# Gates through DRAM, attention A between the gate products, attention B with transposed scores

## The chip, the cores and the metric

One Trainium2 chip, one core. The metric is the device time of one execution in microseconds; the kernel before is given by the median of three runs.

## What is computed

One residual block, 1024 positions of 1024 numbers, float32. Cut to what matters here:

```python
h = rms_norm(x, g_mix[l])
z = h @ w_in[l]
qa, ka, va, cq, ckv, krope, gates = jnp.split(z, COL_SPLITS, axis=-1)
y_a = swa_sink_attention(...)     # 8 heads of 64, 2 kv heads, window of 2 chunks of 64, sinks
y_b = mla_attention(...)          # 8 heads, q and k of 96, v of 64, chunk-causal softmax over all keys
gt = jax.nn.sigmoid(gates + b_gate[l])                       # two gates of 1024 columns
merged = gt[:, :, 0] * (y_a @ w_branch_a[l]) + gt[:, :, 1] * (y_b @ w_branch_b[l])
x = x + merged @ w_out[l]
x = x + jnp.square(jax.nn.relu(rms_norm(x, g_mlp[l]) @ w_ff1[l])) @ w_ff2[l]
```

## The kernel before

Every engine has a program written out by hand, and semaphores join them. The large products are split: each float32 operand is a high and a low part in fp32r, and `split_products` (L1001) makes three products of them. GpSimd splits the weights (`split`, L583 and L585), ScalarE and VectorE the activations.

The stages follow one another on TensorE. (1) x is normalised and transposed, and z is made in four column chunks. (2) 16 gate tiles of 128 columns, 48 products of 128x512 each, in two pairs of PSUM banks; ScalarE's sigmoid (L831, L842) writes all of them to `gate`, 64 KB per partition of SBUF, and between the first eight it squares z for the norms. (3) 18 groups of four transposes (L1008) make `qaT`, `kaT`, `cqT`, `ckvT`. (4) Attention A: 16 units, one per query tile and kv head: scores (L1138), `maxima` on VectorE (L1513 to L1521), exps on ScalarE (L902), normalisation on GpSimd (L693), transposes of P (L1163), values (L1190). Unit k's scores stand beside unit k-1's transposes and unit k-2's values. (5) Attention B: 64 units, one per head and query tile n: scores of n+1 key tiles in plain f32 (L1148), row maximum (L1529), exp (L908), n+1 transposes of P (L1167, L1174), n+1 products with V (L1194), the division by the row sum (L1560). The heads go in groups of two; `group_step` (L1110, L1112, L1008) projects and transposes q and k of a group, one step in each unit, one group ahead, with GpSimd scaling and rotating (L592, L660 to L685). (6) yB is transposed, and `branches` (L1001) makes 8 pairs of branch tiles of 24 products; VectorE's `merge` multiplies by the gates. (7) Output projection, second norm, feed-forward in 8 groups.

Orders are fixed by the loops over k in each engine's program. The softmax of B subtracts an exact row maximum, per query row on a partition.

## Time and profile before

| | us |
|---|---|
| median of 3 runs (lowest, highest) | 1498.99 (1498.45, 1500.33) |
| profiled execution | 1497.08 |
| its span | 1495.1 |
| TensorE busy | 1439.5 |
| VectorE, ScalarE, GpSimd busy | 533.4, 361.3, 502.3 |
| first branch product starts at | 608.1 |

The span runs from the first to the last instruction of the profiled execution, and the execution's own time is 2.0 us more. A busy TensorE can be one whose products follow each other at less than their best pace, so starts are read beside durations. The granted clock of the span is 0.992 of 2.4 GHz.

### The profile page before, as it was taken

The page shows a single profiled execution, that of the slowest core. Times are in us where ns is not written, and L with a number is a line of the kernel's source. Part 1 is how long each engine was busy: PE and PEld are TensorE (multiplying, and loading weights), DVE is VectorE, ACT ScalarE, POOL GpSimd, SP SyncE. Part 2 cuts the span into 40 slices and gives each one's busy share as a digit, 9 for nine tenths or more (in the row PEclk, how much of TensorE's full clock was granted, in tenths as well). Part 3 has the DMA queues.
Part 4 walks back from the last instruction along what each step waited for, and adds up shares of the span by engine and source line. Part 5 has one row for each costly group of instructions (what it writes and reads, how often), then busy time and mean ns, then how long its engine had stood idle before and what let it go on. Part 6 is the DMA issues. An engine that isn't in the chain of part 4 may idle for free.

```text
span 1495.1 us, 18639 instructions
## 1 busy us (share of the span) xinstructions
PE 1439.5 (96%) x7304; PEld 1202.3 (80%) x7304; DVE 533.4 (36%) x980; ACT 361.3 (24%) x781; POOL 502.3 (34%) x357
## 2 busy tenths in 40 slices
PE   7999999977699999899999999999999999999998
PEld 6998888865488877788888888888888888888887
DVE  5300115068666665555253222122222222222212
ACT  5112211065455554210032102020110202011020
POOL 2330654117243241125407133150513415051320
PEclk9999999998999999999999999999999999999999
DMA  7120121000010000015202112030211203021112
GB/s 228 31 57 14 43 56 42 14 23 1 18 38 2 1 1 29 16 55 181 87 1 81 47 43 71 4 95 14 70 42 39 73 0 98 14 70 42 30 40 98
DMA packets 78390, 71.43 MB, mean 48 GB/s; under 512 B 6784, under 2 KB 69760, under 8 KB 78336
## 3 DMA queue, kind: packets, MB, share of 16 engines
q1 hardware_dynamic: 78192, 70.19, 15.7%
q8 instruction: 34, 0.56, 0.1%
q10 hardware_dynamic: 144, 0.52, 0.1%
q14 instruction: 20, 0.16, 0.0%
HBM read 66.51 MB, written 4.19 MB: 47 GB/s over the span
## 4 chain that ended last, share of the span: by engine, by line
PE 89%; DVE 3%; ACT 2%; issue 2%; POOL 2%; DMA 1%; ACTq 0%; SPq 0%; DVEq 0%; POOLq 0%
PE PS L1001 75%; PE PS L1194 4%; PE PS L1148 4%; PE PS L1008 2%; PE PS L1167 2%; PE PS L1110 1%; ACT scA L902 1%; POOL scA L693 1%; DVE uT_lo L1658 1%; PE PS L1112 1%; PE PS L1174 1%; DMA z_raw<-in_w_in 0%; PE PS L1163 0%; DVE yT_lo L1586 0%; ACT uT_hi L989 0%
## 5 line engine op out<-in xcount | busy, mean ns | idle before, releaser
L583 POOL TENSOR_SCALAR w_hi<-raw 128x1024 fp32r<-128x1024 f32 x64 | 74.5, 1164 | 407.5 <-PE PS L1001 406.1
L1658 DVE TENSOR_TENSOR uT_lo<-relu_sq,uT_hi 128x512 fp32r<-128x512 f32 x64 | 92.4, 1479 | 278.6 <-ACT uT_hi L989 278.6
L975 ACT ACTIVATE relu_t<-PS 128x512 f32<-128x512 f32 x64 | 34.8, 595 | 553.3 <-PE PS L1001 553.3
L1664 DVE TENSOR_TENSOR xr<-PS,xr 128x1024 f32<-128x1024 f32 x64 | 78.4, 1225 | 245.6 <-PE PS L1001 245.6
L585 POOL TENSOR_TENSOR w_lo<-raw,w_hi 128x1024 fp32r<-128x1024 f32 x64 | 159.7, 2496 | 5.3
L1001 PE MATMUL PS<-mT_hi,w_hi 128*128 128x512 f32 x512 | 160.3, 389 | 0.7 <-POOL w_lo L585 0.7
L1001 PE MATMUL PS<-mT_lo,w_hi 128*128 128x512 f32 x512 | 160.3, 389 | 0.0
L1001 PE MATMUL PS<-mT_hi,w_lo 128*128 128x512 f32 x512 | 160.2, 389 | 0.0
L1001 PE MATMUL PS<-w_hi,uT_hi 128*128 128x512 f32 x512 | 158.4, 391 | 1.7 <-DVE uT_lo L1658 1.7
L1001 PE MATMUL PS<-w_lo,uT_hi 128*128 128x512 f32 x512 | 157.8, 389 | 0.0
L1001 PE MATMUL PS<-w_hi,uT_lo 128*128 128x512 f32 x512 | 157.6, 389 | 0.0
L1001 PEld LDWEIGHTS PS<-w_hi,uT_hi 128*128 128x128 f32 x512 | 95.6, 188 | 24.0 <-DVE uT_lo L1658 3.9
L1001 PEld LDWEIGHTS PS<-mT_hi,w_hi 128*128 128x128 f32 x512 | 96.1, 188 | 20.7 <-issue 0.9
L1001 PEld LDWEIGHTS PS<-w_lo,uT_hi 128*128 128x128 f32 x512 | 96.1, 188 | 20.1
L1001 PEld LDWEIGHTS PS<-w_hi,uT_lo 128*128 128x128 f32 x512 | 96.1, 188 | 20.0
L1001 PEld LDWEIGHTS PS<-mT_hi,w_lo 128*128 128x128 f32 x512 | 96.1, 188 | 20.0
L1001 PEld LDWEIGHTS PS<-mT_lo,w_hi 128*128 128x128 f32 x512 | 96.1, 188 | 19.9
L1001 PE MATMUL PS<-hT_hi,gw_hi 128*128 128x512 f32 x256 | 79.0, 389 | 0.5 <-ACT Zr L797 0.5
L1194 PEld LDWEIGHTS PS<-vB,ptB 128*128 128x128 f32 x576 | 71.3, 191 | 9.7 <-ACT ptB L921 6.4
L1001 PE MATMUL PS<-hT_lo,gw_hi 128*128 128x512 f32 x256 | 78.8, 389 | 0.0
L1001 PE MATMUL PS<-hT_hi,gw_lo 128*128 128x512 f32 x256 | 78.8, 389 | 0.0
L1001 PE MATMUL PS<-zw_hi,hT_hi 128*128 128x320 f32 (+1 forms) x256 | 77.9, 304 | 0.0
(194 smaller groups left out, 2384.8 us busy)
## 6 DMA issues: line engine op xcount, KB each, us to landing
raw<-in_w_ff SPq DMA_DIRECT2D x64, 512.0 KB, 3.8
g_raw<-in_w_in SPq DMA_DIRECT2D x16, 512.0 KB, 3.8
x_in<-in_x SPq DMA_DIRECT2D x8, 512.0 KB, 10.7
raw<-in_w_out SPq DMA_DIRECT2D x8, 512.0 KB, 3.5
xr<-in_x SPq DMA_DIRECT2D x8, 512.0 KB, 7.6
out<-xr SPq DMA_DIRECT2D x8, 512.0 KB, 2.6
z_raw<-in_w_in SPq DMA_DIRECT2D x4, 640.0 KB, 8.1
z_raw<-in_w_in SPq DMA_DIRECT2D x4, 544.0 KB, 3.8
```

The costliest lines, as they stand in the source:

```text
L583: pool.tensor_scalar(hi_ap, raw_ap, 1.0, 1.0, ALU.mult, ALU.mult).then_inc(hi_done, 1)
L585: pool.tensor_tensor(lo_ap, raw_ap, hi_ap, ALU.subtract).then_inc(ready, 1)
L693: pool.tensor_tensor(p, p, bcast(r, [P, A_GROUP, WIN]), ALU.mult).then_inc(p_normed, 1)
L902: ins = act.activation(scA[:, s, g, 0:WIN + 1], scA[:, s, g, 0:WIN + 1], ACT.Exp, bias=a_nmax[:, s, g:g + 1], accum_out=a_sum[:, ss, g:g + 1])
L975: act.activation(relu_t[:, cols], PS[:, 2 * (j % 2) + h, :], ACT.Relu).then_inc(relu_ready, 1)
L1001: ins = pe.matmul(o, st, cut(mv), start=first and n == 0, stop=last and n == 2)
L1008: ins = pe.transpose(PS[0:rows, bank, i * P:(i + 1) * P], ap, ident[:, :])
L1148: ins = pe.matmul(pair(2 * s)[:, c:c + w], qbT[gs][0:QK, h, n * P:(n + 1) * P], kbT[gs][0:QK, h, c:c + w], start=True, stop=True)
L1167: ins = pe.transpose(PS[:, 4, c * P:(c + 1) * P], prB[s][:, c * P:(c + 1) * P], ident[:, :])
L1194: ins = pe.matmul(PS[:, 6, 0:V_DIM], ptB[s][:, c, :], vB[(m // B_GROUP) % 3][:, c, m % B_GROUP, :], start=c == 0, stop=c == n)
L1658: dve.tensor_tensor(uT_lo[:, j, cols], relu_sq[:, cols], uT_hi[:, j, cols], ALU.subtract).then_inc(uT_ready, 1)
L1664: dve.tensor_tensor(xr[:, t, :], pair(4 + 2 * (t % 2)), xr[:, t, :], ALU.add).then_inc(x3_added, 1)
```

## The change

Two stages are woven and one is turned.

- **Gates through DRAM.** `gate` is two buffers of 4 KB per partition; SP stores each tile to `gate_store` in DRAM and fetches it back for the branches. From the fifth gate tile on all use one pair of PSUM banks (`gate_pair`), so the others are free for what is woven in.
- **Attention A and the first head group lie between the gate products.** The 16 gate tiles are cut into 64 points of 12 products. After a point come two small transposes (points 18 to 26), a step of A (28 to 46), a step of the first group (47 to 59) or three approximate scores of head 0 (60 to 63).
- **Attention B in slots.** A head has 12 slots: query half 0 with key tiles 0 to 3, half 1 with key tiles 0 to 7. `scores_t` makes scores with keys on partitions and up to 512 queries along the row, as three fp32r products of split q and k; a 97th row (ones in k, the negative row maximum in q) subtracts the maximum. Exp writes P in the layout that `values_t` takes, so nothing is transposed: V (with a column of ones, which gives the row sums) is the weights, P is moved. The maxima come a head ahead from `approx`, a single fp32r product in the natural layout, through `row_max` and four DMAs that lay a column of 128 numbers into a row. Per half the row sums go by DMA to a column, VectorE takes reciprocals, and two DMAs spread them through DRAM to 64 rows.
- **Branches.** The 16 tiles go in the order `ORDER`, with four of A first, one tile of 24 products each. yB needs no transposes.

The core of the diff:

```diff
--- before.py
+++ after.py
...
-N_B = B_HEADS * T
-N_UNITS = N_A + N_B
-BG_UNITS = B_GROUP * T
+Q_BLOCK = 4
+BLOCKS = B_HEADS * T // Q_BLOCK
+HEAD_SLOTS = Q_BLOCK + T
+N_SLOTS = B_HEADS * HEAD_SLOTS
+P_RING = 3
+S_RING = 2
+KQ_RING = 4
+SC_RING = 3
+BW_RING = 4
+POINTS = 4
+SMALL_AT = 18
+A_AT = 28
+PROJ_AT = 47
+TURN_AT = 56
+SHIFT_AT = 60
...
+        def gate_pair(u):
+
+            return 0 if u in (1, 3) else 5
+
...
+        def a_step(p):
+
+            return p - A_AT if 0 <= p - A_AT < N_A + 3 else None
+
+        def first_group(p):
+
+            if 0 <= p - PROJ_AT < T:
+                return [p - PROJ_AT]
+            if 0 <= p - TURN_AT < T // 2:
+                return [T + 2 * (p - TURN_AT), T + 2 * (p - TURN_AT) + 1]
+            return []
+
+        def first_chunks(p):
+
+            q = p - SHIFT_AT
+            return [3 * q, 3 * q + 1, 3 * q + 2] if 0 <= q < N_CHUNKS // 3 else []
+
...
+        def preparations(t):
+
+            h, r = t // HEAD_SLOTS, t % HEAD_SLOTS
...
+            def nmax_move(u):
+
+                h, half = u // 2, u % 2
+                with nc.allow_non_contiguous_dma(reason="128 numbers from a column to a row"):
+                    for i in range(Q_BLOCK):
+                        n = Q_BLOCK * half + i
+                        if half == 0:
+                            sp.wait_ge(approx_read, N_CHUNKS * h + i + 1)
+                        else:
+                            sp.wait_ge(nmax_ready, Q_BLOCK * h + i + 1)
+                        sp.dma_start(qT_hi[h % KQ_RING][QK:QK + 1, n * P:(n + 1) * P].bitcast(F32), b_nmax[:, u % 2, i:i + 1]
+                                     ).then_inc(nmax_landed[u % 2], 16)
...
+            def sum_move(u):
+                sp.wait_ge(y_raw_ready, u + 1)
+                sp.dma_start(b_sum[:, u % 2, :], sum_row(u).rearrange("o (p t) -> o p t", t=Q_BLOCK)
+                             ).then_inc(sum_landed[u % 2], 16)
+
+            def reciprocal_spread(u):
+                s, r = u % 2, V_DIM * ((u // 2) % 2)
+                sp.wait_ge(rsum_b_ready, u + 1)
+                sp.dma_start(r_d[s], b_rsum[:, s, :]).then_inc(r_stored, 16)
+                sp.wait_ge(r_stored, 16 * (u + 1))
+                sp.dma_start(r_row[s][r:r + V_DIM, :],
+                             r_d[s].rearrange("p t -> (p t)").rearrange("(o q) -> o q", o=1).partition_broadcast(V_DIM)
+                             ).then_inc(r_landed[s], 16)
...
+            def exp_b(t):
+                h, half, kt, c0 = slot(t)
+                act.wait_ge(st_done, t + 1)
+                before = p_tile_before(t)
+                if before >= 0:
+                    act.wait_ge(slot_done, before + 1)
+                p, sc = p_tile(t), PS[:, 2 + t % S_RING, :]
+                if diagonal(t):
+                    act.activation(p[0:CHUNK, c0:c0 + CHUNK], sc[0:CHUNK, c0:c0 + CHUNK], ACT.Exp)
+                    act.activation(p[:, c0 + CHUNK:HALF], sc[:, c0 + CHUNK:HALF], ACT.Exp).then_inc(p_ready, 1)
                 else:
...
+            def y_out(u):
+
+                odd = (u // 2) % 2
+                act.wait_ge(slot_done, block_end(u))
+                if u >= 2:
+                    act.wait_ge(yB_ready, u - 1)
+                dst, src = y_raw[u % 2], PS[:, 5 + u % 2, :]
+                if odd:
+                    act.activation(dst[0:1, :], src[V_DIM:V_DIM + 1, :], ACT.Copy)
+                    act.activation(dst[V_DIM:P, :], src[0:V_DIM, :], ACT.Copy).then_inc(y_raw_ready, 1)
+                else:
...
+            def y_high(u):
+
+                h, half = u // 2, u % 2
+                rows, cols = slice(V_DIM * (h % 2), V_DIM * (h % 2) + V_DIM), slice(half * HALF, (half + 1) * HALF)
+                act.wait_ge(y_normed, u + 1)
+                act.activation(yT_hi[4 + h // 2][rows, cols], y_raw[u % 2][rows, :], ACT.Copy).then_inc(yB_hi_done, 1)
...
+            def approx(a):
+
+                h, n, c, w = chunk(a)
+                q, k = qT_hi[h % KQ_RING], kT_hi[h % KQ_RING]
+                if n == 0 and h % B_GROUP == 0:
+                    pe.wait_ge(qk_ready, T * (h // B_GROUP + 1))
+                if a == 0:
+                    pe.wait_ge(max_ready, N_A)
+                if a >= 2:
+                    pe.wait_ge(approx_read, a - 1)
+                pe.matmul(PS[:, a % 2, 0:w], q[0:QK, n * P:(n + 1) * P], k[0:QK, c:c + w], start=True, stop=True
+                          ).then_inc(approx_done, 1)
+
+            def scores_t(t):
+
+                h, half, kt, c0 = slot(t)
+                s = h % KQ_RING
+                keys, cols = slice(kt * P, (kt + 1) * P), slice(half * HALF + c0, (half + 1) * HALF)
+                if t == 0:
+                    pe.wait_ge(k_one_ready, KQ_RING)
+                if kt == 0:
+                    u = 2 * h + half
+                    pe.wait_ge(nmax_landed[u % 2], 16 * Q_BLOCK * (u // 2 + 1))
+                if t >= S_RING:
+                    pe.wait_ge(p_ready, t - S_RING + 1)
+                out = PS[:, 2 + t % S_RING, c0:HALF]
+                pe.matmul(out, kT_hi[s][0:QK + 1, keys], qT_hi[s][0:QK + 1, cols], start=True, stop=False)
+                pe.matmul(out, kT_hi[s][0:QK, keys], qT_lo[s][0:QK, cols], start=False, stop=False)
+                pe.matmul(out, kT_lo[s][0:QK, keys], qT_hi[s][0:QK, cols], start=False, stop=True
+                          ).then_inc(st_done, 1)
+
+            def values_t(t):
+
+                h, half, kt, c0 = slot(t)
+                u, g = 2 * h + half, h // B_GROUP
+                last = t + 1 == block_end(u)
+                pe.wait_ge(p_ready, t + 1)
+                if kt == 0 and u >= 2:
+                    pe.wait_ge(y_raw_ready, u - 1)
+                if t % (2 * HEAD_SLOTS) == 0 and g < 3:
...
+                    pe.wait_ge(p_zero_ready, Q_BLOCK)
+                ins = pe.matmul(out[:, c0:HALF], vB[g % 3][:, kt, h % B_GROUP, :], p_tile(t)[:, c0:HALF],
+                                start=kt == 0, stop=last)
+                ins.then_inc(slot_done, 1)
+
+            def gate_chunks(u, q):
+                b = gate_pair(u)
+                if q == 0:
+                    pe.wait_ge(gw_ready, u + 1)
+                    before = [v for v in range(u) if gate_pair(v) == b]
+                    if before:
+                        pe.wait_ge(gate_ready, before[-1] + 1)
+                for k in range(2 * q, 2 * q + 2):
+                    ins = split_products(gw_hi[u % 2][:, k, :], gw_lo[u % 2][:, k, :], hT_hi[:, k, :], hT_lo[:, k, :],
+                                         [(PS[:, b + h, :], halves[h]) for h in range(2)], k, k == 0, k == KD - 1)
+                if q == POINTS - 1:
+                    ins.then_inc(gate_done, 1)
+
+            for p in range(2 * KD * POINTS):
+                gate_chunks(p // POINTS, p % POINTS)
+                for n in small_at(p):
+                    small_transpose(n)
+                k = a_step(p)
+                if k is not None:
+                    if 2 <= k < N_A + 2:
+                        p_transposes(k - 2, 0)
+                    if k < N_A:
+                        scores(k)
+                    if k >= 3:
+                        values(k - 3)
+                    if 2 <= k < N_A + 2:
+                        p_transposes(k - 2, 1)
+                for q in first_group(p):
+                    group_step(0, q)
+                for a in first_chunks(p):
...
+            for t in range(N_SLOTS):
+                scores_t(t)
+                if t >= 2:
+                    values_t(t - 2)
+                a = chunk_at(t)
+                if a is not None:
+                    approx(a)
+                for g, p in preparations(t):
+                    group_step(g, p)
+            values_t(N_SLOTS - 2)
+            values_t(N_SLOTS - 1)
...
+            def row_max(a):
+
+                h, n, c, w = chunk(a)
+                u, i = 2 * h + n // Q_BLOCK, n % Q_BLOCK
+                dve.wait_ge(approx_done, a + 1)
+                if u >= 2 and i == 0 and c == 0:
+                    dve.wait_ge(nmax_landed[u % 2], 16 * Q_BLOCK * (u // 2))
+                sc = PS[:, a % 2, 0:w]
+                if c + w == (n + 1) * P:
+                    link(dve, dve.memset(sc[0:CHUNK, w - CHUNK:w], -MASKED))
+                out = b_nmax[:, u % 2, i:i + 1]
...
+            def y_norm(u):
+                rows, _ = block_rows(u)
+                dve.wait_ge(r_landed[u % 2], 16 * (u // 2 + 1))
+                dve.tensor_tensor(y_raw[u % 2][rows, :], y_raw[u % 2][rows, :], r_row[u % 2][rows, :], ALU.mult
+                                  ).then_inc(y_normed, 1)
+
+            def y_low(u):
+                rows, cols = block_rows(u)
+                j = 4 + u // 4
+                dve.wait_ge(yB_hi_done, u + 1)
+                dve.tensor_tensor(yT_lo[j][rows, cols], y_raw[u % 2][rows, :], yT_hi[j][rows, cols], ALU.subtract
+                                  ).then_inc(yB_ready, 1)
...
```

Where the instructions move, at three places.

TensorE in attention A: a unit before (transposes of P from `scA`, scores from `qaT` and `kaT`, a projection of the first group, values from `ptA`).

```order
L1190 MATMUL PS<-ptA,v_even 128x256 [waits y_ready,pt0_ready]
L1190 MATMUL PS<-ptA,Zr 128x256
L1163 MATMUL PS<-ident,scA 128x64 [waits p_normed,pt0_ready,exp_done]
L1163 MATMUL PS<-ident,scA 128x64 x7
L1138 MATMUL PS<-kaT,qaT 128x192 [waits max_ready]
L1138 MATMUL PS<-kaT,qaT 128x192 x3
L1110 MATMUL PS<-wuq,cqT 128x192 [waits proj_dve_read,proj_act_read]
L1110 MATMUL PS<-wuq,cqT 128x192
```

Now, the same unit, with a point of gate products (`gw` times `hT`) behind it.

```order
L1375 MATMUL PS<-ident,scA 128x64 [waits p_normed,pt0_ready,exp_done]
L1375 MATMUL PS<-ident,scA 128x64 x3
L1360 MATMUL PS<-kaT,qaT 128x192 [waits max_ready]
L1360 MATMUL PS<-kaT,qaT 128x192 x3
L1389 MATMUL PS<-ptA,v_even 128x256 [waits y_ready,pt0_ready]
L1389 MATMUL PS<-ptA,Zv 128x256
L1375 MATMUL PS<-ident,scA 128x64 [waits pt_half]
L1375 MATMUL PS<-ident,scA 128x64 x3
L1245 MATMUL PS<-hT_hi,gw_hi 128x512 x2
L1245 MATMUL PS<-hT_lo,gw_hi 128x512 x2
L1245 MATMUL PS<-hT_hi,gw_lo 128x512 x2
```

The projections have left the unit, the transposes are two halves around scores and values, and gate products stand before the next.

ScalarE in attention A before: projections' reads, `ptA`, exps.

```order
L902 ACTIVATE scA,a_sum<-scA,a_nmax 128x193 [waits max_ready]
L902 ACTIVATE scA,a_sum<-scA,a_nmax 128x193 x3
L879 ACTIVATE q_nat<-PS 128x192 [waits proj_done]
L882 ACTIVATE sqB<-PS 128x448 [waits b_summed]
L917 ACTIVATE ptA<-PS 128x512 [waits pt0_done]
L902 ACTIVATE scA,a_sum<-scA,a_nmax 128x193 [waits max_ready]
```

Now, around the end of a gate tile.

```order
L1118 ACTIVATE scA,a_sum<-scA,a_nmax 128x193 [waits max_ready]
L1118 ACTIVATE scA,a_sum<-scA,a_nmax 128x193 x3
L1048 ACT_TABLE_LOAD [waits gate_stored1]
L1048 ACTIVATE gate<-PS,b_gate_c 128x1024 [waits gate_done]
L1126 ACTIVATE ptA<-PS 128x512 [waits pt0_done]
L1118 ACT_TABLE_LOAD
L1118 ACTIVATE scA,a_sum<-scA,a_nmax 128x193 [waits max_ready]
L1118 ACTIVATE scA,a_sum<-scA,a_nmax 128x193 x3
L1126 ACTIVATE ptA<-PS 128x512 [waits pv_done,pt0_done]
```

A sigmoid stands between the exps of two units, with a table load ahead of it and one behind.

SP's queue in attention B, of a head (before, it held nothing there but the loads of two weights a group).

```order
L649 DMA b_sum<-y_raw 128x1x4 [waits y_raw_ready]
L639 DMA qT_hi<-b_nmax 1x128x1 [waits approx_read] x4
L655 DMA r_store<-b_rsum 128x4 [waits rsum_b_ready]
L657 DMA r_row<-r_store 64x512 [waits r_stored]
L639 DMA qT_hi<-b_nmax 1x128x1 [waits nmax_ready] x4
L649 DMA b_sum<-y_raw 128x1x4 [waits y_raw_ready]
L655 DMA r_store<-b_rsum 128x4 [waits rsum_b_ready]
L657 DMA r_row<-r_store 64x512 [waits r_stored]
L649 DMA b_sum<-y_raw 128x1x4 [waits y_raw_ready]
```

VectorE at the same time, one half block.

```order
L1823 TENSOR_REDUCE b_part<-PS 128x1 [waits nmax_landed1,approx_done]
L1832 RECIPROCAL b_rsum<-b_sum 128x4 [waits r_stored,sum_landed1]
L1817 MEMSET PS 64x64 [waits approx_done]
L1823 TENSOR_REDUCE b_part<-PS 128x1 [waits dve_step]
L1826 TENSOR_TENSOR b_nmax<-b_part 128x1 [waits approx_read]
L1823 TENSOR_REDUCE b_part<-PS 128x1 [waits approx_done]
L1842 TENSOR_TENSOR y_raw<-y_raw,r_row 64x512 [waits r_landed1]
L1817 MEMSET PS 64x64 [waits approx_done]
L1823 TENSOR_REDUCE b_part<-PS 128x1 [waits dve_step]
```

The maxima, the sums and the reciprocals of a head all go through SP in this order, and VectorE's multiply by `r_row` stands in its queue ahead of later row maxima.

## Rows read from the trace of the kernel before

**Rows 1.** The page: busy time, and the chain that ended last by engine.
```profile
PE 1439.5 (96%) x7304; PEld 1202.3 (80%) x7304; DVE 533.4 (36%) x980; ACT 361.3 (24%) x781; POOL 502.3 (34%) x357
...
PE 89%; DVE 3%; ACT 2%; issue 2%; POOL 2%; DMA 1%; ACTq 0%; SPq 0%; DVEq 0%; POOLq 0%
```

**Rows 2.** Windows, four stages; columns: width, then busy us (instructions) per engine, clock, DMA.
```profile
127.00:301.40 174.40, 174.25 (x769) 144.23 (x770) 33.93 (x95) 29.32 (x36) 69.97 (x32) 1.00 0.14 36
301.40:401.20 99.80, 69.72 (x478) 51.37 (x476) 74.21 (x199) 58.03 (x183) 43.36 (x44) 0.90 0.05 13
401.20:601.50 200.30, 196.17 (x1293) 161.39 (x1293) 121.53 (x406) 105.48 (x253) 62.20 (x70) 0.99 0.05 15
...
608.10:1495.10 887.00, 880.17 (x3904) 726.98 (x3904) 262.18 (x214) 127.54 (x234) 289.52 (x164) 1.00 0.18 55
```

**Rows 3.** Timeline, TensorE, attention A; columns: start us, us, line, operation, idle before.
```profile
312.85 1.65 PE L1138 MATMUL PS<-kaT,qaT 64*128 64x192 f32 x8 [2.02 <-DVE ckvT L1439]
...
341.85 0.47 PE L1163 MATMUL PS<-ident,scA 64*128 64x64 f32 x8 [1.03 <-POOL scA L693]
...
343.26 0.89 PE L1110 MATMUL PS<-wuq,cqT 128*128 128x192 f32 x4 [0.23 <-DVE vB L1476]
...
346.61 0.47 PE L1163 MATMUL PS<-ident,scA 64*128 64x64 f32 x8 [0.90 <-POOL scA L693]
```

**Rows 4.** Timeline, TensorE: z stage, small transposes, attention B, output products.
```profile
119.86 0.29 PE L1001 MATMUL PS<-zw_lo,hT_hi 128*128 128x272 f32 x1
119.99 0.28 PE L1001 MATMUL PS<-zw_hi,hT_lo 128*128 128x272 f32 x1
...
301.38 1.91 PE L1008 MATMUL PS<-ident,Zq 128*128 128x128 f32 x16
303.12 1.04 PE L1008 MATMUL PS<-ident,k_dup 128*128 128x128 f32 x8
...
560.40 0.66 PE L1167 MATMUL PS<-ident,prB 128*128 128x128 f32 x4 [0.55 <-ACT prB L908]
...
577.25 1.88 PE L1148 MATMUL PS<-kbT,qbT 96*128 96x512 f32 x4
578.97 0.56 PE L1194 MATMUL PS<-vB,ptB 128*128 128x64 f32 x4
...
581.95 0.66 PE L1167 MATMUL PS<-ident,prB 128*128 128x128 f32 x4 [0.55 <-ACT prB L908]
...
775.00 0.71 PE L1001 MATMUL PS<-ow_hi,mT_hi 128*128 128x512 f32 x2
```

**Rows 5.** Groups by line and shape, 110 to 610 us; busy us, mean ns of one.
```profile
L585 POOL TENSOR_TENSOR gw_lo<-g_raw,gw_hi 128x1024 fp32r<-128x1024 f32 x14 | 33.9, 2424 | 1.2
...
L902 ACT ACTIVATE scA<-scA,a_nmax 128x193 f32<-128x193 f32 x64 | 28.2, 444 | 0.0
...
L592 POOL TENSOR_TENSOR b_rstd<-b_ms,minus_half 128x16 f32<-128x16 f32 x8 | 23.3, 2913 | 90.9 <-DVE b_ms L1500 90.9
...
L1529 DVE TENSOR_REDUCE b_nmax<-PS 128x1 f32<-128x512 f32 x8 | 5.5, 691 | 0.3
```

**Rows 6.** Timeline, ScalarE, around the first gate tile.
```profile
138.44 1.28 ACT L831 ACT_TABLE_LOAD   x1 [9.51 <-PE PS L1001]
139.73 1.12 ACT L831 ACTIVATE gate<-PS,b_gate_c 128x1024 f32<-128x1024 f32 x1
```

**Rows 7.** DMA issues (KB, us to landing), then SP's queue (start, us of issue).
```profile
raw<-in_w_ff SPq DMA_DIRECT2D x64, 512.0 KB, 3.8
...
pos_i<-in_positions SPq DMA_DIRECT2D x1, 4.0 KB, 14.2
...
g_ckv_c<-in_g_ckv SPq DMA_DIRECT2D x1, 0.5 KB, 2.2
...
7.60 3.21 SPq L463 DMA_DIRECT2D pos_i<-in_positions  x1
...
20.92 0.47 SPq L463 DMA_DIRECT2D g_ckv_c<-in_g_ckv  x1
```

More of the change, by code:

```diff
@@ L302, in build @@
         g_mlp_in = sem("g_mlp_in")
-        xr_landed = [sem(f"xr_landed{t}") for t in range(T)]
         o_done = sem("o_done")
@@ L397, in kind @@
         def kind(k):
[L399 to L415 removed]
+            return k // 2, k % 2
         def yT_cols(k, odd):
[L419 removed]
+            m, n = kind(k)
             rows = slice(CHUNK * odd, CHUNK * odd + CHUNK)
@@ new lines, in scores @@
+                    pe.wait_ge(max_ready, k - 1)
+                for g in range(A_GROUP):
+                    head = A_GROUP * n + g
+                    r = A_DIM * (head % 2)
+                    ins = pe.matmul(PS[:, 2 * s + g % 2, 256 * (g // 2):256 * (g // 2) + WIN],
+                                    qaT[r:r + A_DIM, head // 2, m * P:(m + 1) * P],
+                                    kaT[r:r + A_DIM, n, m * P:m * P + WIN], start=True, stop=True)
+                ins.then_inc(qk_done, 1)
@@ new lines, in scores_t @@
+            def scores_t(t):
+                h, half, kt, c0 = slot(t)
+                s = h % KQ_RING
[12 more added lines that the diff above has]
+                          ).then_inc(st_done, 1)
@@ L1241, in out_tile @@
+            for e in range(2 * KD):
+                branch(e)
             def out_tile(n):
@@ L1417, in _ @@
             dve.wait_ge(rope_ready, 2)
-            with dve.Fori(0, T // 2) as i:
+            for i in range(T // 2):
                 z_norms(i, False)
@@ new lines, in maxima @@
+                if k == 0:
+                    dve.wait_ge(dist_ready, 3)
+                if k >= SC_RING:
+                    dve.wait_ge(pt0_done, k - SC_RING + 1)
+                for g in range(A_GROUP):
+                    dve.scalar_tensor_tensor(out=sc[:, g, 0:WIN], in0=dist[:, m, :],
+                                             scalar=-SLOPES[A_GROUP * n + g],
+                                             in1=PS[:, 2 * s + g % 2, 256 * (g // 2):256 * (g // 2) + WIN],
+                                             op0=ALU.mult, op1=ALU.add)
@@ new lines, in _ @@
+            dve.wait_ge(gate_done, 2 * KD)
+            for i in range(2, KQ_RING):
+                dve.memset(kT_hi[i][QK:QK + 1, :].bitcast(F32), 1.0).then_inc(k_one_ready, 1)
+            for i in range(Q_BLOCK):
+                dve.memset(p_diag[i][CHUNK:P, i * P:i * P + CHUNK], 0.0).then_inc(p_zero_ready, 1)
+            for t in range(N_SLOTS):
+                a = chunk_at(t)
+                if a is not None:
+                    row_max(a)
+                for g, p in preparations(t):
+                    group_vec(g, p)
+                for u in range(BLOCKS):
+                    if t == block_end(u) + 4:
+                        sum_reciprocal(u)
+                    if t == block_end(u) + 6:
+                        y_norm(u)
+                    if t == block_end(u) + 8:
+                        y_low(u)
@@ L1611, in x2_norm, with merged_low @@
+            def merged_low(d):
+                dve.wait_ge(mT_hi_done, d + 1)
+                dve.tensor_tensor(mT_lo[:, d, :], gate_b[:, d, :], mT_hi[:, d, :], ALU.subtract).then_inc(mT_ready, 1)
+            for e in range(2 * KD):
+                gate_multiply(e)
+                if ORDER[e][0] and ORDER[e][1]:
+                    merged_low(ORDER[e][1] - 1)
+            merged_low(KD - 1)
             def x2_norm(t):
```

1074 lines of the change are left out of this document (555 added, 519 removed).

## The prediction, made before the change was run

> **What bounds the kernel now.** I read the page first: TensorE is busy 96% of the span, and the chain that ended last lies on it for 89% [rows 1]. So the time changes only by work taken off TensorE or by gaps on it. The stages say where gaps are [rows 2]: the gate products (127 to 301 us) and all from the branch products to the end (608.1 to 1495.1 us) are full, while attention A fills 69.7 of 99.8 us at a mean granted clock of 0.90, and attention B fills 196.2 of 200.3 us. The timeline of A shows the gap [rows 3]: transposes of one unit start at 341.85 and of the next at 346.61, so a unit takes 4.76 us, with about 1 us of it idle until GpSimd's normalisation (L693) is done. After a wait of 2.02 us the scores take 1.65 us, where transposes and scores together otherwise take 1.4 (341.85 to 343.26): that is the lower of the two clocks, 1.2 GHz.
>
> From the end of the z stage to the first branch product before is 608.1 - 127.0 = 481.1 us [rows 2]. All of the change falls there. From 608.1 on, the same number of products at the same shapes is left (887 us), and I cost that at nothing: gates come back from DRAM as 16 loads of 512 KB under 87 us of products; such a load lands in 3.8 us [rows 7].
>
> **Prices of TensorE's work.** Split products (fp32r) of 512 columns: 174.4 us hold 769, so 0.2267 us each [rows 2]. Of 272 columns: 0.125 us from start to start [rows 4]. Both are N/2.4 ns and 12 ns more, so I take 0.173 for 384 and 0.120 for 256. For 128 there is no row; between 0.066 (this formula) and 0.11 (a full-rate transpose: 16 in 1.74 us [rows 4]) I take 0.10, since a weight load of the same size precedes both. Plain f32 with 512+512 columns takes 1.72 us from start to start (577.25 to 578.97 [rows 4]), so 0.86 per 512, four times the columns.
>
> **Attention B per head.** Before: eight units, 4608 columns of f32 scores (7.7 us), 36 transposes (3.9) and 36 products with V, each two short instructions at a transpose's price (7.9): 19.5 us, and 21.55 with waits (560.40 to 581.95 [rows 4]). After: 12 slots. The scores are 6 pieces of 512 and two each of 384, 256, 128, three times in fp32r: 18 x 0.227 + 6 x (0.173 + 0.120 + 0.10) = 6.4 us. V moves to the weights' side, P is moved, in f32: the same 4608 columns, 7.8 us. The maximum needs an approximate score in natural layout: 12 products, 2.2 us. Sum 16.4 us, so 3.1 less of work per head; the 36 transposes are gone, and with them yB's 32 (3.5 us).
>
> **The sum of TensorE's work after**, between z and branches: gates 174.1; 72 small transposes 7.9; 16 units of A at 2.1 and 32 projections at 1.16 (a unit with its projection is 4.76 less 0.90 of wait in front of the transposes and some 0.6 in small waits [rows 3]: 3.26) 33.6 and 37.1; 128 transposes of q and k 14.1; B 8 x 16.4 = 131. Together 397.8. The same list before is 426.3, with 156 for B and 3.5 for yB. So 28.5 us of work go, and 481.1 - 426.3 = 55 us of gaps stand against whatever the change leaves.
>
> **The gaps that stay, stage by stage.** The order rows show a unit of A after every quarter of a gate tile: 12 products x 0.2267 = 2.72 us in front of 2.1 us of A, 4.8 us in all, so DVE's link copy, exps (four at 0.44 [rows 5]) and GpSimd's 1.47 us have two such points, 9.6 us, where they had one unit. This cover holds.
> - Before the first small transpose (point 18, at 127 + 19 x 2.72 = 179): it waits for gate tile 3's sigmoid, which stands on ScalarE behind half of `dist`, and that behind the zeroed border, which stands on GpSimd behind the split of gate tile 5 (allowed when tile 3 is done, 127 + 16 x 2.72 = 170.5; a split takes some 3.6 us, its second half 2.42 [rows 5]). Then 1.5 + 1.9 + 1.1 us on ScalarE: about 182. Gap 3 us.
> - From gate tile 4 on there is one PSUM pair, so the next tile waits for the sigmoid of the last. The sigmoid takes 1.12 us [rows 6]. Where about 0.9 to 1.2 us of other work stand between, the gap is 0.3; where none does (points 27 and 55), 1.3. In A, exps of the unit before run until 0.6 us after the tile, then the table load (1.28) and the sigmoid (1.12): ready at 3.1, side work 2.1, gap 1.0, four times. Together 9 us. The trace shows the table load as 1.28 us with no pause on either side [rows 6].
> - The Trainium skill ("ScalarE: Activation LUTs", What ACT_TABLE_LOAD costs) gives 2.66 us per switch, 1.38 of it a drain, and its rules say to do all of one table set before switching, which this change does not. By that the four gaps would be 2.4 us each and the time some 6 us longer; the row has no drain, so I go by the row.
> - q and k of the first group at point 58 wait for GpSimd (power 2.9 [rows 5], scaling and rotation some 6.4, behind a split of 3.6): 2 us. Three approximate scores per point with two banks and 0.69 us per reduction of 512 [rows 5]: 3 us. Small waits in A: 2.
> - The slots begin with the maxima moved to a row. SP reaches these only after the last gate store (sigmoid 1.2), then four issues at 0.47 us and a landing of 2.2 [rows 7], 5.6 in all, with 1.3 of work under it: gap 4.3.
> - Head 0 carries 16 preparations, and GpSimd needs 9.3 us for each half: 5 us.
> - The chain of a block's sums: y_raw, to a column, reciprocal, to DRAM, wait, back to 64 rows; each of the three transfers taken as the small load's 2.2 us and a tenth for the issue. DVE's multiply, six slots on, waits for it about 2 us, then ScalarE's high half, which holds up the exps. In heads with preparations a slot is 1.9 us and this is covered; in the last three it costs 0.7 us for each of six blocks: 4 us.
> - Weight loads that a short product can't cover (the pair right after transposes lasts 0.71 us [rows 4], where 0.389 + 0.227 = 0.62 is the rule, 0.09 more): about 100 places, 9 us. Low clock after the two long gaps: 3 us, as in [rows 3].
>
> Sum 3+9+2+3+2+4+5+4+9+3 = 44. Behind it nothing waits at the branches: they open with A's four tiles (21.8 us), and the last block needs some 16 us for its sums even behind three gate loads.
>
> Result: 397.8 + 44 = 441.8 against 481.1, so -39.3 us, plus nothing later. The profiled execution took 1497.1 us (2.0 around its span), 1.9 below the median of the runs; from the execution the forecast is 1457.8, and **I say 1458**.
>
> **Rivals.**
> - *Few gaps.* The weights' changeovers are hidden (in B before, waits and changeovers together were only 2 us a head) and the chain of sums is covered: 20 us of gaps, 1434. For: B before ran within 4 us of full over 200 [rows 2]. Against: six new cross-engine loops.
> - *ScalarE holds the gates.* If behind each of the nine tiles from the seventh on ScalarE is late by a table load, exps and sigmoid in full (1.28 + 1.8 + 1.1 = 4.2 us, of which 1.1 are in my sum), the gates lose 28 us: 1486. For: one PSUM pair and the switch of tables between exps. Against: the load waits only for the store of an older tile, so it runs ahead where ScalarE is idle.
> - *The small transfers hold the slots; slower than before.* The maxima go as 128 pieces of 4 bytes, eight times a head, on the same queue as the sums. A load of 1024 such pieces took 14.2 us to land and held the queue 3.21 us [rows 7]. If four of 128 cost half of that landing, one after another with the sums, a head takes 2 x 7.1 + 2 x 7.1 = 28.4 us where I have about 22: 8 x 6.4 = 51, so 1509. It decides from 5 us per head on, which is a landing of some 4 us for each step. Against: one of 128 pieces landed in 2.2 us.
> - The Trainium skill ("DMA: Bandwidth & Descriptors", Specifications) says that below 512 B a transfer does a read-modify-write and loses line rate. That speaks for this last rival; the 2.2 us row says that at this size it doesn't matter for the landing.
>
> **How the numbers follow.** Forecast 0.62 (its own range 1444 to 1472); few gaps 0.20; ScalarE 0.11; transfers 0.07. Most unknown terms are gaps, so I take 1434 to 1484 as the range, leaving out the slow rival and the ends of others. A measurement of this kernel can tell about 0.2% (3 us) from no change. Faster by more: the first three and a little of the last, 0.93; same 0.02; slower 0.05.
>
> **What would show it.** First branch product at about 568 us of the span, 887 us before the end. Gate stage with A: some 250 us, TensorE over 93% busy, clock 1.0. A head without preparations at 17 to 18 us. Scores of 512 columns 0.227 apart, products with V of 512 at 0.86. Waits of TensorE on `gate` sigmoids: 9 us; on p (exps): under 8. SP's moves of b_nmax at about 0.5 us of issue. Wrong if a quiet head takes over 20 us, if the gate stage takes over 265, or if TensorE waits at the fifth branch tile.

## The result, and the profile after the change

The changed kernel takes 1479.45 us (median of 4 runs, 1477.18 to 1484.96) where the kernel before takes 1499.66 (4 runs, 1498.45 to 1500.50): a ratio of 0.9871, 95% interval 0.9843 to 0.9900. It is faster, by 20 us where 39 were forecast. The profiled execution is the longest of the four, 1484.96 us with a span of 1483.2, so its own distance from the forecast is 27 us, and I account for those.

| | before | after | forecast |
|---|---|---|---|
| median, us | 1499.66 | 1479.45 | 1458 |
| profiled execution, us | 1497.1 | 1484.96 | 1457.8 |
| first branch product at | 608.1 | 596.2 | 568 |
| from there to the end | 887.0 | 887.0 | 887 |

The page, as in [rows 1] (busy time, then the chain that ended last by engine and by line):

```profile
PE 1426.6 (96%) x6792; PEld 1164.7 (79%) x6792; DVE 539.3 (36%) x947; ACT 367.8 (25%) x811; POOL 526.0 (35%) x381
...
PE 81%; DVE 6%; DMA 5%; POOL 3%; ACT 2%; issue 2%; SPq 0%; DVEq 0%; ACTq 0%; POOLq 0%
PE PS L1245 73%; DMA r_row<-r_store 3%; PE PS L1439 2%; PE PS L1252 1%; DMA r_store<-b_rsum 1%; PE PS L1389 1%; DVE uT_lo L1962 1%; PE PS L1338 1%; DVE b_part L1823 1%; PE PS L1375 1%; PE PS L1360 1%; ACT gate L1048 1%; DVE y_raw L1842 1%; PE PS L1403 1%; POOL b_rstd L781 1%
```

TensorE is busy for 13 us less, as wanted, but has left the chain for 8 more per cent of the span. What came in its place are DVE, GpSimd and DMA, and among the DMAs two of this change: the reciprocals' way through DRAM, `r_store` and `r_row`. The windows (width, then busy us and instructions of TensorE, weight loads, DVE, ScalarE, GpSimd; granted clock; DMA), as in [rows 2], for the gates with A, head 0, heads 1 to 7, and the rest:

```profile
127.00:393.80 266.80, 248.37 (x1252) 194.98 (x1252) 120.14 (x329) 104.19 (x232) 117.44 (x76) 0.99 0.19 60
393.80:429.00 35.20, 31.43 (x146) 24.33 (x147) 20.89 (x66) 15.98 (x43) 22.67 (x25) 0.90 0.08 14
429.00:596.00 167.00, 151.06 (x659) 103.66 (x657) 102.70 (x280) 83.34 (x225) 57.70 (x58) 0.94 0.12 20
596.00:1483.20 887.20, 880.46 (x3907) 727.14 (x3905) 260.12 (x213) 129.23 (x236) 291.03 (x176) 1.00 0.21 66
```

The last row is the same as before. The third isn't what I foresaw: 16 us idle, and a clock of 0.94. The longest waits of TensorE behind the z stage (us in total, times, longest):

```profile
PE PS L1403 <- DVE b_part L1823: 11.1, 7, 2.6
PE PS L1245 <- ACT gate L1048: 6.9, 8, 2.6
PE PS L1252 <- POOL q_nat L883: 5.4, 3, 2.7
PE PS L1419 <- DMA qT_hi<-b_nmax: 4.2, 1, 4.2
PE PS L1419 <- ACT p_diag L1152: 3.3, 1, 3.3
PE PS L1403 <- DVE kT_lo L1764: 2.6, 1, 2.6
```

The first (9.8 of its 11.1 us; the rest lies in the gate stage) and the fifth are one thing, a wait of TensorE once in each of the heads 2 to 7: 2.42, 1.28, 1.09, 2.35, 2.63 and 3.29 us. It is seen here at the turn from head 5 to head 6. First TensorE's timeline (start us, us, line, operation, idle before and its releaser), then DVE's, ScalarE's and SP's:

```profile
554.29 0.41 PE L1403 MATMUL PS<-kT_hi,qT_hi 96*128 96x128 f32 x1
554.54 0.39 PE L1419 MATMUL PS<-qT_hi,kT_hi 97*128 97x384 f32 x1
...
555.12 0.38 PE L1439 MATMUL PS<-p_diag,vB 128*65 128x128 f32 x2
558.14 0.58 PE L1403 MATMUL PS<-kT_hi,qT_hi 96*128 96x256 f32 x1 [2.63 <-DVE b_part L1823]
...
559.43 1.91 PE L1439 MATMUL PS<-p_diag,vB 128*65 128x512 f32 x2
```

```profile
551.27 0.16 DVE L1832 RECIPROCAL b_rsum<-b_sum 128x4 f32<-128x4 f32 x1
...
552.38 0.69 DVE L1823 TENSOR_REDUCE b_part<-PS 128x1 f32<-128x512 f32 x1
556.55 0.69 DVE L1842 TENSOR_TENSOR y_raw<-y_raw,r_row 64x512 f32<-64x512 f32 x1 [3.48 <-DMA r_row<-r_store]
557.25 0.11 DVE L1817 MEMSET PS<- 64x64 f32 x1
557.40 0.69 DVE L1823 TENSOR_REDUCE b_part<-PS 128x1 f32<-128x512 f32 x1
```

```profile
557.27 0.63 ACT L1174 ACTIVATE yT_hi<-y_raw 64x512 fp32r<-64x512 f32 x1 [4.29 <-DVE y_raw L1842]
557.92 0.22 ACT L1151 ACTIVATE p_diag<-PS 64x64 f32<-64x64 f32 x1
```

```profile
551.46 0.33 SPq L655 DMA_DIRECT2D r_store<-b_rsum  x1
552.87 0.48 SPq L657 DMA_DIRECT2D r_row<-r_store  x1
```

From the reciprocal (551.27) to the multiply (556.55) pass 5.3 us: 1.6 until the reciprocals are stored in DRAM and their way back is issued (552.87), then 3.7 until 64 rows of them have landed (medians of the two landings: 1.4 and 3.4). DVE stands at the multiply for 3.48 us, and what is queued behind it are the maxima of the approximate scores; TensorE has two banks for those and stops at the third, 2.63 us. ScalarE stands at the high half, with the exps behind it. DVE waits like this at both blocks of a head (15 times, 40.9 us in all), but TensorE stops behind only one of them. Then, from 558.14, TensorE runs at half clock (granted clock 0.50 from 558 to 562): two products with V take 1.91 us where the same form takes 1.02 at full clock. The DMA rows (KB, median us to landing), the small load of [rows 7] being my measure for all of them:

```profile
r_row<-r_store SPq DMA_DIRECT2D x16, 128.0 KB, 3.4
...
qT_hi<-b_nmax SPq DMA_DIRECT2D x64, 0.5 KB, 2.1
...
b_sum<-y_raw SPq DMA_DIRECT2D x16, 2.0 KB, 2.0
r_store<-b_rsum SPq DMA_DIRECT2D x16, 2.0 KB, 1.4
```

### The profile page after: what moved, and what is told of

Its sections match the earlier page's. It is cut to its first block, busy times and chain, and to the rows that moved or that the text cites. A ratio compares the mean times of both kernels' runs of the same rounds, so it can differ in the third digit from the quotient of the medians.

```text
span 1483.2 us, 17278 instructions
## 1 busy us (share of the span) xinstructions
PE 1426.6 (96%) x6792; PEld 1164.7 (79%) x6792; DVE 539.3 (36%) x947; ACT 367.8 (25%) x811; POOL 526.0 (35%) x381
## 4 chain that ended last, share of the span: by engine, by line
PE 81%; DVE 6%; DMA 5%; POOL 3%; ACT 2%; issue 2%; SPq 0%; DVEq 0%; ACTq 0%; POOLq 0%
PE PS L1245 73%; DMA r_row<-r_store 3%; PE PS L1439 2%; PE PS L1252 1%; DMA r_store<-b_rsum 1%; PE PS L1389 1%; DVE uT_lo L1962 1%; PE PS L1338 1%; DVE b_part L1823 1%; PE PS L1375 1%; PE PS L1360 1%; ACT gate L1048 1%; DVE y_raw L1842 1%; PE PS L1403 1%; POOL b_rstd L781 1%
## 5 line engine op out<-in xcount | busy, mean ns | idle before, releaser
L1245 PE MATMUL PS<-hT_hi,gw_hi 128*128 128x512 f32 x256 | 85.3, 415 | 9.1 <-ACT gate L1048 6.9
L1245 PE MATMUL PS<-zw_hi,hT_lo 128*128 128x320 f32 (+1 forms) x256 | 77.0, 301 | 0.0
## 6 DMA issues: line engine op xcount, KB each, us to landing
x_in<-in_x SPq DMA_DIRECT2D x8, 512.0 KB, 10.5
```

The costliest lines, as they stand in the source:

```text
L1245: ins = pe.matmul(o, st, cut(mv), start=first and n == 0, stop=last and n == 2)
```

## The experiments

Twelve runs, in three sets; those of a set share a chip and the runs of the kernel before. Ratios are to that kernel, with 95% intervals.

**The multiply moved to later and earlier slots.** The edit in `e1_late` (ScalarE's high half, then DVE's multiply and low half; the tails after the loops accordingly). `e2_later7` has multiply, high and low half at 7, 8 and 9, `e3_soon5` at 5, 6 and 8:

```
-                    if t == block_end(u) + 7:
+                    if t == block_end(u) + 9:
                         y_high(u)
...
-                    if t == block_end(u) + 6:
+                    if t == block_end(u) + 8:
                         y_norm(u)
-                    if t == block_end(u) + 8:
+                    if t == block_end(u) + 10:
                         y_low(u)
...
```

Expected of `e1_late`: 

> The multiply of a block by its reciprocals is issued 8 slots after the block's end in place of 6 (high half at 9, low half at 10). Theory 1 (the trip of the sums): from reciprocal to multiply the two transfers take 5.4 us where two quiet slots are 3.5, and DVE and ScalarE stand still meanwhile, so that TensorE waits in a head's second slot and then runs at half clock. Four slots cover it: waits on r_row near 0, heads 5 to 7 at 17 to 18.5 us in place of 21.4, 22.8 and 20.1, head 2 at 21 in place of 25.9, TensorE's waits on b_part and p_diag under 2 us in all; 11 to 16 us off the changed kernel, so about 1466. Theory 2 (the waits are only where a lack of work on TensorE collects; slots are set by products and scores with their changeovers): the idle time moves to other slots, a quiet head stays above 20 us, 0 to 4 us off.

Expected of `e2_later7`: 

> The same with the multiply 7 slots after the block's end. Theory 1: three slots are 4.8 to 5.5 us against the 5.4 of the trip, so nearly all goes: within 4 us of the run with 8 slots, about 1468. Theory 2: 0 to 3 us off the changed kernel.

Expected of `e3_soon5`: 

> The multiply 5 slots after the block's end, one slot less than the change. Theory 1: each of 15 waits grows by a slot of 1.7 to 2.3 us, nothing covers it in quiet heads, part in the others: 12 to 28 us slower than the changed kernel, about 1498, and waits on r_row above 50 us. Theory 2: at most 3 us slower.

Measured: 8 slots 1463.25 us (0.9768, 0.9751 to 0.9786); 7 slots 1465.43 (0.9783, 0.9764 to 0.9802); 6 slots, the change, 0.9871; 5 slots 1509.63 (1.0072, 1.0048 to 1.0095), slower than the kernel before. One slot earlier costs 30 us (12 to 28 were expected), one later gives 14, and 7 and 8 slots can't be told apart. Theory 2 has no room for either step. The runs move the multiply and the high half together, so they don't say how much of it is DVE's wait and how much ScalarE's. The windows of `e1_late`, the first two and the third, which holds the same 659 products as that of the changed kernel:

```profile
127.00:393.80 266.80, 248.37 (x1252) 194.96 (x1252) 120.14 (x329) 104.19 (x232) 117.43 (x76) 0.99 0.19 60
393.80:429.00 35.20, 31.41 (x146) 24.30 (x147) 20.41 (x67) 15.98 (x43) 22.65 (x25) 0.90 0.09 14
429.00:576.70 147.70, 141.74 (x659) 97.84 (x657) 102.48 (x279) 84.15 (x225) 57.95 (x58) 1.00 0.14 22
```

Up to 429 us the two executions agree to 0.02 us of TensorE's time. Behind it 19.3 us are gone: 10.0 of idle time (15.94 to 5.96) and 9.3 of busy time (151.06 to 141.74) for the same products, by the clock alone, 0.94 to 1.00. So in this pair of executions the half clock doubles what the waits cost. It didn't follow each of them: behind the 2.42, 2.35, 2.63 and 3.29 us of heads 2, 5, 6 and 7 it came (granted clock of these heads 0.87, 0.92, 0.85, 0.92), behind the 1.28 and 1.09 us of heads 3 and 4 it didn't (1.00), and neither behind a wait of 2.57 us for `kT_lo` in head 1 (1.00). Heads 5, 6 and 7, from first score to first score (head 7: to the first branch product), take 17.7, 17.2 and 15.7 us (21.4, 22.8 and 20.1 in the changed kernel). The same turn of heads in `e1_late`, DVE; the maxima go on ahead of the multiply, whose wait is now short. Over the whole kernel DVE still waits 18.6 us for the row, where I expected near 0, but 15.9 of these belong to the last three blocks, which no maxima stand behind; TensorE's waits on `b_part` are 3.2 us, where I expected under 2:

```profile
540.93 0.68 DVE L1843 TENSOR_TENSOR y_raw<-y_raw,r_row 64x512 f32<-64x512 f32 x1 [0.23 <-DMA r_row<-r_store]
...
547.14 0.69 DVE L1843 TENSOR_TENSOR y_raw<-y_raw,r_row 64x512 f32<-64x512 f32 x1 [1.26 <-DMA r_row<-r_store]
```

With 5 slots DVE's waits for the row, over the whole kernel, are what was foreseen (above 50; 40.9 with 6 slots):

```profile
DVE y_raw L1842 <- DMA r_row<-r_store: 67.9, 16, 6.2
```

**The same two kernels again, on one chip.** `e10_same` is the changed kernel unaltered, `e11_late_again` is `e1_late`.

Expected of `e10_same`: 

> The changed kernel as it is, beside the two that follow on the same chip. About 0.987 of the kernel before, 1478. If the half clock behind a wait comes by chance (after the same 2.57 us wait at gate tile 8 it came in one profile and stayed away in two others), the waits stand where they stood and are as long to 0.1 us, but the stretches of half clock differ, by some 2 to 6 us in the span.

Expected of `e11_late_again`: 

> The run with the multiply 8 slots after the block's end once more, on the chip on which the changed kernel itself is timed too. Theory 1: 14 to 18 us below the changed kernel; theory 2: under 4.

Measured: 1481.80 us (0.9881, 0.9858 to 0.9904) and 1462.40 (0.9766, 0.9745 to 0.9786). The move of the multiply is worth 19 us by the medians, a little more than the 14 to 18 expected. And the half clock behind a wait comes in one execution and not in another. The end of the wait for gate tile 7's sigmoid, first in the changed kernel's profile, then in `e10_same`, two products each line:

```profile
237.79 1.19 PE L1245 MATMUL PS<-hT_hi,gw_hi 128*128 128x512 f32 x2 [2.57 <-ACT gate L1048]
238.78 1.06 PE L1245 MATMUL PS<-hT_lo,gw_hi 128*128 128x512 f32 x2
```

```profile
237.29 0.70 PE L1245 MATMUL PS<-hT_hi,gw_hi 128*128 128x512 f32 x2 [2.57 <-ACT gate L1048]
237.84 0.63 PE L1245 MATMUL PS<-hT_lo,gw_hi 128*128 128x512 f32 x2
```

The same wait, to the hundredth, costs 2.57 us in `e10_same` and 5.2 in the changed kernel's profile (from the first of the twelve products to the unit of A behind them 5.39 us, not 2.94, and 0.20 more on the unit). That fits the changed kernel's runs lying 8 us apart and those of `e1_late` 4. Not all waits are as long in both, though: that for `kT_lo` in head 1 is 2.57 us in one and 0.26 in the other, that in head 3 1.28 and 1.79. The Trainium skill ("TensorE: Matmul & The Clock Gate", Part 1: The HAM clock gate) says of the slow stretch at a kernel's start that its length differs from run to run of one kernel; these two profiles differ in the same way behind a wait in the middle.

**Attention A apart.** `e4_apart` runs all gate tiles first, then A and the first head group; `e12_filled` adds products that nobody reads ahead of each unit.

```
-A_AT = 28
-PROJ_AT = 47
-TURN_AT = 56
-SHIFT_AT = 60
+A_AT = 64
+PROJ_AT = 83
+TURN_AT = 92
+SHIFT_AT = 96
...
```

The loops over the points run to 100 in all four engines' programs, with gate products in the first 64. In `e12_filled` TensorE also has:

```
+                elif p < 64 + N_A + 1:
+                    if p == 64:
+                        pe.wait_ge(gate_ready, 2 * KD)
+                    for i in range(8):
+                        pe.matmul(PS[:, 5 + i % 2, :], gw_hi[1][:, i % KD, :], hT_hi[:, i % KD, 0:HALF],
+                                  start=True, stop=True)
```

Expected of `e4_apart`: 

> Attention A and the first head group behind the gate tiles (all gate tiles first), the rest as in the change. If interleaving hides waits between engines, as the prediction has it: a unit of A takes 3.5 us or more where it takes 2.8 between gate products (16 units: 11 us or more), each gate tile from the fifth waits 1.3 us for its sigmoid (8 or more tiles more than now: 10 us), low clock in A 4 us, less 4 us for the gaps of table loads: 18 to 30 us slower than the changed kernel, about 1503, near the kernel before. Rival (the transposes already stand two units behind, so that a unit alone has no gap; the gain of the change is all in attention B): at most 10 us slower, all of it the sigmoids.

Expected of `e12_filled`: 

> Attention A behind the gates as before, but with eight fp32r products of 512 columns, whose result nobody reads, ahead of each unit of A on TensorE (17 units, 1.8 us each at full clock). With A apart a unit took 5.40 us, 4.6 of it TensorE at half clock. If what interleaving buys is the clock (theory C): the clock stays at or near full, a unit takes 4.5 to 4.7 us in spite of the added work, A ends 10 to 15 us earlier than with A apart, 1540 in all. If it buys cover for waits between engines (my prediction): the added 1.8 us fill the waits of 0.8 us and the rest comes on top, at half clock 8 us a unit, 20 to 40 us slower than with A apart, 1580.

Measured: 1552.57 us (1.0357, 1.0332 to 1.0382) and 1547.60 (1.0331, 1.0307 to 1.0355). Taking the interleaving back costs 73 us, far above both expectations: without it the change would be a loss of 54. That is the price of this order taken apart, not of interleaving alone: from A's first scores to attention B the kernel before takes 88.4 us (312.85 to 401.20), with the first group's projections between A's units, and `e4_apart` 132.4 (327.6 to 460.0), with the first group behind A. The slots begin at 460.0, not 393.8. Of these 66 us 41 are A: from its first scores to the first projection it takes 85.5 us (327.6 to 413.1), where its parts between gate products sum to 42 and 2.7 us of changeovers. Of the other 25 some 6 are sigmoids (TensorE waits 12.5 us for them in all, where it waits 6.9 in the changed kernel), the rest is the first group, whose chain has nothing beside it (waits for GpSimd of 5.9 and 4.9 us). A unit of A in `e4_apart`, then in `e12_filled`:

```profile
363.85 0.55 PE L1375 MATMUL PS<-ident,scA 64*128 64x64 f32 x3 [0.73 <-issue]
...
364.31 1.59 PE L1360 MATMUL PS<-kaT,qaT 64*128 64x192 f32 x7
365.82 1.22 PE L1389 MATMUL PS<-ptA,v_even 128*128 128x256 f32 x2
...
369.25 0.55 PE L1375 MATMUL PS<-ident,scA 64*128 64x64 f32 x3 [0.73 <-issue]
```

```profile
364.77 2.14 PE L1463 MATMUL PS<-hT_hi,gw_hi 128*128 128x512 f32 x8
366.83 0.40 PE L1375 MATMUL PS<-ident,scA 64*128 64x64 f32 x3
...
367.13 0.87 PE L1360 MATMUL PS<-kaT,qaT 64*128 64x192 f32 x7
...
369.38 2.14 PE L1463 MATMUL PS<-hT_hi,gw_hi 128*128 128x512 f32 x8
```

And the windows of the two over the same 68 us:

```profile
342.00:410.00 68.00, 53.92 (x269) 36.94 (x268) 45.62 (x121) 32.16 (x119) 20.54 (x14) 0.65 0.00 1
```

```profile
342.00:410.00 68.00, 63.80 (x388) 45.51 (x388) 48.15 (x124) 34.38 (x126) 21.16 (x15) 1.00 0.01 1
```

With the added products the clock is 1.00 instead of 0.65, and 119 more instructions fit into the same time. So the added work costs no time, which theory C says and mine doesn't. But C's 10 to 15 us didn't come: not all units of `e4_apart` are as slow as the one I had read. From the third unit's scores to the last's (334.8 to 397.6) they average 4.83 us; three at full clock take 3.6, 3.7 and 4.0. Filled, they average 4.73, nearly all of it TensorE's work (63.8 of 68 us). The whole kernels lie 5 us apart, and their intervals overlap. From 2.8 us between gate products, some 0.8 to 1.2 us of a unit apart are thus waits that full clock leaves, and about as much is the clock.

**Four smaller places**, each on top of `e1_late`. `e5_nmax` issues `nmax_move(0)` before the last gate store and lets the first scores wait for two of the four rows of ones; `e6_aearly` has A_AT = 27 and PROJ_AT = 46; `e7_first` has FIRST = (0, 0, 1, 1, 2, 2, 3, 4, ...); `e8_all` has all three; `e9_best` has the first and the third, and sets the other two rows of ones in slots 5 and 6.

```
             for u in range(2 * KD):
+                if u == 2 * KD - 1:
+                    nmax_move(0)
                 sp.wait_ge(gate_ready, u + 1)
...
-            nmax_move(0)
             nmax_move(1)
...
                 if t == 0:
-                    pe.wait_ge(k_one_ready, KQ_RING)
+                    pe.wait_ge(k_one_ready, 2)
+                if t == 2 * HEAD_SLOTS:
+                    pe.wait_ge(k_one_ready, KQ_RING)
```

Expected of `e5_nmax`: 

> On top of the run with the multiply at 8: the first four maxima of head 0 go to their row before the last gate store, not behind it, and the first scores wait for the ones in two key tiles, not four. Theory of the start (a wait for landing 4.2 us long, and the half clock that it brings): the wait at 393.9 goes or falls under 1 us, the first head starts near 390, its first slot takes 2.2 in place of 3.4 us: 5 us off, 1458 where the run it stands on took 1463. Rival (the next thing in line is as late: the table load for exp ends at 390.6, the first 16 preparations wait for GpSimd): head 0 only shifts its wait to its slots 10 and 11; 0 to 2 us off.

Expected of `e6_aearly`: 

> On top of the run with the multiply at 8: attention A and the projections of its first group begin one quarter of a gate tile earlier, so that the tile's end without side work (a wait of 1.3 us) has some, and the first exps are through before gate tile 7's sigmoid. If the 2.57 us wait there, with the half clock behind it (5.1 where 2.9 us are usual for twelve products), is a matter of start-up: all of it goes, 5 to 7 us off, 1457. Rival (ScalarE's table load and sigmoid behind exps hold one tile of four in any case): the wait only moves to another tile, 0 to 1.5 us off.

Expected of `e7_first`: 

> On top of the run with the multiply at 8: head 0's projections of the next group stand one or two slots earlier. If GpSimd, which is busy without pause from 405.8 on (2 x 9.4 us), is what TensorE waits for in head 0's slot 10 and head 1's slot 0 (2.7 + 2.3 us and half clock after both): GpSimd starts 3 us earlier, both waits fall below 1 us, 5 to 7 us off, 1457. Rival (the chain in front of GpSimd, ScalarE's and DVE's reads of each projection, sets the pace): projections wait for their two banks instead, GpSimd starts less than 1 us earlier, -1 to +3 us.

Expected of `e8_all`: 

> The three edits together, on top of the multiply at 8. If they are separate waits, their gains add: 12 to 18 us off the 1463 of the run they stand on, 1448. If what one frees the next takes back, 1456 or more.

Expected of `e9_best`: 

> The multiply at 8, the first maxima ahead of the last gate store, and head 0's projections earlier, with the ones of two key tiles set in slots 5 and 6; attention A stays where it is, since beginning it earlier gave nothing. If the start of the slots and GpSimd's start are separate waits: 1453 to 1455, 2 to 4 us below the run without the last edit (0.9732 of the kernel before). If the earlier projections only wait for their two banks: 1457.

Measured:

| run | us | ratio | interval |
|---|---|---|---|
| e5_nmax | 1456.96 | 0.9732 | 0.9719 to 0.9746 |
| e6_aearly | 1463.58 | 0.9764 | 0.9751 to 0.9778 |
| e7_first | 1460.80 | 0.9752 | 0.9739 to 0.9765 |
| e8_all | 1455.67 | 0.9721 | 0.9708 to 0.9734 |
| e9_best | 1455.20 | 0.9717 | 0.9697 to 0.9737 |

The start of the slots was a wait of its own: 4.21 us before the first scores in the changed kernel, none in `e5_nmax`, and full clock in its place (in the changed kernel the starts are 0.54 and 0.42 us apart, in `e5_nmax` 0.23 and 0.24):

```profile
393.85 0.74 PE L1419 MATMUL PS<-qT_hi,kT_hi 97*128 97x512 f32 x1 [4.21 <-DMA qT_hi<-b_nmax]
394.39 0.63 PE L1420 MATMUL PS<-qT_lo,kT_hi 96*128 96x512 f32 x1
394.81 0.63 PE L1421 MATMUL PS<-qT_hi,kT_lo 96*128 96x512 f32 x1
```

```profile
386.39 0.39 PE L1423 MATMUL PS<-qT_hi,kT_hi 97*128 97x512 f32 x1
386.62 0.39 PE L1424 MATMUL PS<-qT_lo,kT_hi 96*128 96x512 f32 x1
386.86 0.39 PE L1425 MATMUL PS<-qT_hi,kT_lo 96*128 96x512 f32 x1
```

Beginning A earlier gave nothing: the wait for the tile's sigmoid only fell from 2.57 to 1.92 us, again with half clock behind it, and two new waits of 0.4 to 0.5 for GpSimd came, as the rival had it. Earlier projections gave less than half of what I expected: GpSimd begins 3.5 us earlier (402.31, not 405.78), but its 18.9 us then run on, and TensorE, further along too, waits 2.52 us for it where it waited 2.70. The three together give 7.6 us by the medians, not 12 to 18. `e9_best` is the fastest that I ran, 42 us below the kernel before on its chip and 27 below the changed kernel; from `e8_all` it can't be told apart.

## Why the prediction was right and wrong

The direction, the range and the place were right; of the 39 us forecast, half was missing. By its own steps, in the profiled execution (27 us short):

- **Behind the first branch product nothing changes.** Right, 887.0 us both times; the gates from DRAM cost nothing.
- **B takes 16.4 us of work per head.** Right. With the chain of sums covered, a quiet head takes 17.2 to 17.7 us in `e1_late`, and one without any wait 16.6 (head 6 of `e9_best`). In the changed kernel itself the forecast of 17 to 18 us failed (20.1 to 22.8), and by my own test (over 20) it counts as wrong. By the other test (gate stage over 265) it does too: 266.8 us up to the first scores.
- **The chain of a block's sums, 4 us. This step failed**, and it is most of the error: 19.3 us in the profile, 19 by the medians on one chip. The mechanism stood there, down to who waits for whom. It wasn't the landings: three at 2.2 us were forecast, 6.6 in all, and 2.0, 1.4 and 3.4 were measured, 6.8. DVE's wait was put at about 2 us and was 2.1 to 3.7 in heads 5 to 7, wherever maxima stand behind it. What failed is what was made of it. TensorE's share was put at 0.7 us for each of six blocks, as if what stands behind DVE's multiply had slack of a slot; it has two PSUM banks, and TensorE waits once a head, 2.35 to 3.29 us in these three. The half clock behind these waits was left out, which cost nearly as much again (9.3 of 19.3). And heads with preparations were taken as covered: heads 2, 3 and 4 have the wait as well (2.42, 1.28 and 1.09 us), and head 2 lost 3.2 us to it.
- **A unit of A takes 2.1 us.** Too low: its parts between gate products take 2.64, so 8.6 us more in 16 units. I had taken 0.6 us of "small waits" out of [rows 3], which show 0.23: 4.76 less 0.90 and 0.23 is 3.63, and 2.64 for the unit, 0.89 for the projection and 0.1 for changeovers make that. The projection in turn was priced too high (1.16, where eight take 0.89: 2.2 us in the other direction).
- **Changeovers, 9 us at about 100 places.** In the wrong place. The twelve gate products behind side work take 2.82 to 2.96 us and not 2.72; without waits and low clock all 768 take 181 us where I had 174.1, so 7 us in the gate stage. In B the head without a wait takes 16.6 us where the work alone was put at 16.4: 0.2 a head and not 1. Heads with preparations weren't taken apart.
- **Waits in the gate stage, 19 us.** 14.2 came: 6.9 on sigmoids (9 forecast), 1.5 at the first small transpose and 1.8 for split weights ahead of it (3), 1.7 for q of the first group (2), 2.4 at head 0's approximate scores (3), none inside A (2). The ScalarE rival fell: only tile 7's sigmoid came later than forecast, the others cost 0.2 to 1.3 us. The table load shows no drain: exps end at 235.22, load 235.24 to 236.52, sigmoid at 236.53. By the Trainium skill ("ScalarE: Activation LUTs", What ACT_TABLE_LOAD costs) there would have been one of 1.38 us; the trace disagrees.
- **Start of the slots, 4.3 us.** 4.21, and removing it gave 5 to 6 us; the half clock behind it went too. **Head 0, 5 us:** 1.0 and 2.7, with 2.6 more at the start of head 1.
- **Low clock, 3 us. This term failed too:** 9.3 in heads 1 to 7, 2.6 at gate tile 8, and more in head 0 at a mean clock of 0.90. I had allowed for it behind two long gaps only; most of it came behind the waits for the chain of sums.

With the 9 us of changeovers counted in the slots and the 3 us of low clock ahead of them, the terms give 256.3 us up to the first scores and 185.5 from there to the branches. Measured were 266.8 and 202.3, 10.5 and 16.8 over. Of the 10.5 the terms above explain 8.2 (8.6 + 7 - 2.2 - 4.8 - 0.4); the rest stays open. `e1_late` needs 183.0 us from first scores to branches: with the sums covered, that part of the forecast holds to 2.5 us, though its terms were off both ways. The transfers' rival had the right culprit for the wrong transfer: the maxima land in 2.1 us and hold up no slot after the first in the changed kernel (one for 0.6 us in `e1_late`), while the sums do; at 5 slots it becomes real, on the slower side (1.0072).

What is left open: why full clock follows the same 2.57 us wait in one execution and not in another. A shorter way for the reciprocals than through DRAM wasn't tried, and why the row takes 3.4 us to land wasn't tested. The price of the A unit, the projection and the changeovers is read from the trace and wasn't tested by a run.

## What to carry to other kernels

An instruction that waits for a transfer belongs as many slots behind its trigger as the transfer takes at the *shortest* slots of the kernel, not the mean ones: here one slot more gave 14 us, one less cost 30. In a forecast, price such a wait by what is queued behind it on its engine and how many buffers that has, and where it makes a dense TensorE stand still as long as here (2.35 to 3.3 us), allow up to as much again for the clock; behind 1.1 and 1.3 us nothing was added here. Work whose steps wait on other engines pays doubly by itself, in waits and in clock; between dense products A's own steps paid neither (the one long wait there was the gate products', for a sigmoid).
